# One branch around the overflow blocks, two norms from one pass of squares, and shifts on four buffers

## The reference, cut to what matters

```python
h = h + hier_moe(rms_norm(h, norm2_gain[l]), ...)      # end of the first block
x = rms_norm(h, final_gain)                            # EPS = 1e-6
# second block, for each of its two layers
shift, scale, gate = split(silu(c) @ w_mod + b_mod, 3)
hh = rms_norm_2(x, g, 1e-6) * (1.0 + scale) + shift
y = short_conv_mixer(hh, ...)        # layer 0: four projections, a 3-wide convolution, gates
y = dilated_mixer(hh, ...)           # layer 1
x = x + gate * y
```

## Time and profile before

| | us |
|---|---|
| median of 3 runs | 1616.34 (1616.0 to 1616.87) |
| the profiled execution's own time | 1616.23 |
| its span, first to last instruction | 1614.1 |
| PE busy in the span | 1447.2 (90%) |
| DVE busy | 705.7 (44%) |
| ACT busy | 488.8 (30%) |

### The profile page before, as it was taken

One profiled execution on the slowest core, in us unless ns is written; L12 is line 12 of the kernel. 1 busy time (PEld: TensorE's weight loads), 2 busy tenths in 40 slices (PEclk: granted clock), 3 DMA queues, 4 the chain that ended last, 5 costly groups with the idle time before them and its releaser, 6 DMA issues.

```text
span 1614.1 us, 18013 instructions
## 1 busy us (share of the span) xinstructions
PE 1447.2 (90%) x6858; PEld 1006.7 (62%) x6858; DVE 705.7 (44%) x1297; ACT 488.8 (30%) x723; POOL 38.6 (2%) x73
## 2 busy tenths in 40 slices
PE   6999997999898988898818999998999999999986
PEld 5786776444443433343216888776888888888765
DVE  4567737211011021010054756455256666666635
ACT  6462532110010100010043222324244445444532
POOL 2010000000000000000020110000000000000000
PEclk9999997999999999999959999998999999999988
DMA  8737335699999964999873553121212121121101
GB/s 355 310 131 263 139 119 209 276 426 426 427 426 427 427 268 163 391 423 429 351 296 131 196 208 131 65 80 53 105 53 105 53 85 73 52 105 52 53 1 65
DMA packets 36811, 336.88 MB, mean 209 GB/s; under 512 B 4560, under 2 KB 4688, under 8 KB 18384
## 3 DMA queue, kind: packets, MB, share of 16 engines
q1 hardware_dynamic: 29632, 304.69, 47.0%
q0 software_dynamic: 6624, 29.89, 5.2%
q10 hardware_dynamic: 432, 0.60, 0.1%
HBM read 312.62 MB, written 22.54 MB: 208 GB/s over the span
## 4 chain that ended last, share of the span: by engine, by line
PE 51%; DVE 2%; issue 2%; ACT 2%; DMA 2%; POOL 0%; DVEq 0%; SPq 0%; ACTq 0%; POOLq 0%
PE ps L290 50%; DMA spare<-in_wts_dram 1%; PE ps L718 1%; ACT ar L860 1%; DVE b_NL L1293 0%; PE ps L296 0%; DMA ar<-y_scratch,rt 0%; DVE ar L1285 0%; ACT b_NH L869 0%; DVE ar L1959 0%; DVE ar L1244 0%; DVE hres L1769 0%; DMA y_scratch<-gate 0%; POOL ar L2035 0%; ACT ar L1214 0%
## 5 line engine op out<-in xcount | busy, mean ns | idle before, releaser
L290 PE MATMUL ps<-ring,ar 128*64 128x512 f32 x800 | 244.3, 610 | 15.8 <-issue 10.7
L290 PE MATMUL ps<-ar 128*64 128x512 f32 (+5 forms) x798 | 231.4, 482 | 18.3 <-DVE ar L1589 6.8
L290 PE MATMUL ps<-b_NH,b_WH 128*128 128x512 f32 x704 | 185.6, 399 | 11.0 <-ACT b_NH L869 5.9
L290 PE MATMUL ps<-b_NH,b_WL 128*128 128x512 f32 x704 | 180.2, 391 | 0.0
L1226 DVE TENSOR_TENSOR b_WL<-ring,b_WH 128x1024 fp32r<-128x1024 f32 x112 | 136.6, 1220 | 94.5 <-ACT b_WH L812 94.5
L290 PE MATMUL ps<-b_NL,b_WH 128*128 128x512 f32 x704 | 174.4, 390 | 0.0
L812 ACT ACTIVATE b_WH<-ring 128x1024 fp32r<-128x1024 f32 x112 | 118.3, 1057 | 161.7 <-PE ps L290 159.9
L290 PEld LDWEIGHTS ps<-ar 128*64 128x64 f32 (+3 forms) x798 | 97.5, 163 | 100.5 <-issue 93.1
L290 PEld LDWEIGHTS ps<-b_NH,b_WH 128*128 128x128 f32 x704 | 129.7, 189 | 39.5 <-ACT b_NH L869 11.7
L290 PEld LDWEIGHTS ps<-ring,ar 128*64 128x64 f32 x800 | 77.8, 140 | 118.6 <-issue 117.0
L290 PEld LDWEIGHTS ps<-b_NH,b_WL 128*128 128x128 f32 x704 | 133.0, 189 | 27.9
(11 more groups left out here) (269 smaller groups left out, 1879.5 us busy)
## 6 DMA issues: line engine op xcount, KB each, us to landing
ring<-in_wts_dram SPq DMA_DIRECT2D x84, 2048.0 KB, 13.6
ar<-in_wts_dram SPq DMA_DIRECT2D x24, 2048.0 KB, 19.4
spare<-in_wts_dram SPq DMA_DIRECT2D x24, 2048.0 KB, 19.0
ring<-in_wmod_dram SPq DMA_DIRECT2D x24, 512.0 KB, 4.9
ar<-in_wmod_dram POOLq DMA_DIRECT2D x24, 512.0 KB, 4.1
y_scratch<-gate POOLq DMA_DIRECT2D x11, 1024.0 KB, 21.3
y_scratch<-gate SPq DMA_DIRECT2D x44, 128.0 KB, 15.7
y_scratch<-ar SPq DMA_DIRECT2D x24, 128.0 KB, 15.9
```

The costliest lines, as they stand in the source:

```text
L290: return pe.matmul(o, l, m, start=start, stop=stop, skip_group_check=True)
```

## The change

Four edits, and what they bring with them.

- **One branch.** On each engine the 12 `If(n_over > j)` go inside one `If(n_over > 0)`.
- **Both norms from one pass of squares.** ACT squares `hres` once for each p into `x0c`. DVE (`products`) multiplies these squares with the squared gain `fgsq` and sums, which gives the second mean without the first norm: 1/rs2 = sqrt(mean(h² g²) + EPS·mean(h²) + EPS²). ACT takes the root of that, DVE inverts it (`both`), and `x0c` is `hres` scaled by it (ACT for p = 0, 1, 2, DVE for p = 3). The final gain is folded into the scale columns (`C_FG`, `fgc`, once, where the columns are made). The first norm of `hres` itself, still wanted for the residual, is made later: four means and inverses ahead of the shift, and the four multiplications (`normed`) between the weight parts of the first panel of the convolution. The memsets of `TT` move behind them.
- **Shifts on four buffers.** `shifted(k)` waits for the low part of k - 4, and is issued two steps ahead. Both uses.
- **`fgr` earlier.** SP loads it behind the store of expert 28; ACT squares it into `fgsq`.

```diff
-            for j in range(NOV):
-                with pe.If(n_over > j):
...
+            with pe.If(n_over > 0):
+                for j in range(NOV):
+                    with pe.If(n_over > j):
+                        overflow(j)
...
             def turned_shift(ops, l, natural, tb, nb, tmps):
                 def shifted(k):
-                    o, src = tmps[k % 2], ps[:, k, :]
+                    o, src = tmps[k % 4], ps[:, k, :]
...
-                    if k >= 2:
-                        act.wait_ge(S["nl"], nb + k - 1)
+                    if k >= 4:
+                        act.wait_ge(S["nl"], nb + k - 3)
...
+                shifted(1)
                 for k in range(8):
-                    if k % 2 == 0:
-                        shifted(k + 1)
-                        act.wait_ge(S["ttd"], 4 * l + k // 2 + 1)
-                    else:
-                        act.wait_ge(S["tta"], 4 * l + k // 2 + 1)
-                    act.activation(ops[0][:, k, :], tmps[k % 2], ACT.Copy).then_inc(S["nh"], 1)
+                    if k % 2 == 1 and k < 7:
+                        shifted(k + 2)
+                    act.wait_ge(S[("ttd", "tta")[k % 2]], 4 * l + k // 2 + 1)
+                    act.activation(ops[0][:, k, :], tmps[k % 4], ACT.Copy).then_inc(S["nh"], 1)
...
+            act.wait_ge(S["fgain"], 16)
...
+            act.activation(fgsq, fgr, ACT.Square).then_inc(S["fgsq"], 1)
...
+            pk_squares(0)
+            pk_squares(1)
+            pk_root(0, rs2, 6)
+            pk_unit(0)
+            pk_squares(2)
+            pk_root(1, rs2, 6)
+            pk_unit(1)
+            pk_squares(3)
+            pk_root(2, rs2, 6)
+            pk_unit(2)
+            pk_root(3, rs2, 6)
+            for p in range(4):
+                pk_root(p, rs, 10)
...
+            def products(p):
+                dve.wait_ge(s_un[p], U_PK + 3)
+                dve.tensor_scalar(eps_s[:, p:p + 1], rs[:, p:p + 1], EPS / D, EPS * EPS, ALU.mult,
+                                  ALU.add).then_inc(s_un[p], 1)
+                dve.tensor_tensor_reduce(out=x0c[:, p, :], in0=x0c[:, p, :], in1=fgsq, scale=1.0, scalar=0.0,
+                                         op0=ALU.mult, op1=ALU.add, accum_out=rs2[:, p:p + 1]).then_inc(s_un[p], 1)
+                dve.wait_ge(s_un[p], U_PK + 5)
+                dve.scalar_tensor_tensor(out=rs2[:, p:p + 1], in0=rs2[:, p:p + 1], scalar=1.0 / D,
+                                         in1=eps_s[:, p:p + 1], op0=ALU.mult, op1=ALU.add).then_inc(s_un[p], 1)
+            def both(p):
+                dve.wait_ge(s_un[p], U_PK + 7)
+                dve.reciprocal(rs2[:, p:p + 1], rs2[:, p:p + 1]).then_inc(s_un[p], 1)
...
             pick(1, 1)
-            norm(0)
+            dve.wait_ge(S["fgsq"], 1)
+            products(0)
             pick(2, 0)
+            both(0)
             pick(2, 1)
-            norm(1)
+            products(1)
             pick(3, 0)
+            both(1)
             pick(3, 1)
+            products(2)
+            both(2)
+            products(3)
+            both(3)
+            dve.wait_ge(s_un[3], U_PK + 8)
+            dve.tensor_scalar(x0c[:, 3, :], hres[:, 3, :], rs2[:, 3:4], None, ALU.mult).then_inc(s_un[3], 1)
+            for p in range(4):
+                mean_square(p, rs, U_PK + 8)
+            for p in range(4):
+                inverse(p, rs, U_PK + 8)
...
+                        if q == 0 and c == 0:
+                            normed(j)
...
+                if n == NE - 4:
+                    sp.wait_ge(S["m_row"], NE // 4)
+                    sp.dma_start(fgr, row(R_FG, 1024)).then_inc(S["fgain"], 16)
```

More of the change, by code:

```diff
@@ L36 @@
 v_w0 v_w1
-cc tt0 xr cv y zc tm
+cc tt0 xr cv y zc tm fgsq fgc
 sw ra rb qk z vk scr att fl pt av
@@ L228, in program @@
         yg = [area(1024 * j, 1024) for j in range(8)]
-        fgr = area(8192, 1024)
+        fgr, fgsq = area(8192, 1024), area(9216, 1024)
+        eps_s = sm[:, 32:36]
         yTc = area(0, 8, 512)
@@ L641, in tensor_program, with overflow @@
             down_main(NE - 1)
[L642 to L659 removed]
+            def overflow(j):
+                if j == 0:
+                    pe.wait_ge(S["t_y"], NE)
+                pe.wait_ge(S["t_oh"], NE + j + 1)
+                pick_third(3).then_inc(S["t_gx"], 1)
+                pe.wait_ge(S["t_xg"], NE + j + 1)
+                turn_third(6).then_inc(S["t_tx"], 1)
+                pe.wait_ge(S["t_xt"], NE + j + 1)
+                pe.wait_ge(S["v_w0"], 32 * j + 16)
+                pe.wait_ge(S["v_w1"], 16 * j + 16)
+                up(xT3, 0, ov).then_inc(S["t_up"], 1)
+                pe.wait_ge(S["t_hh"], NE + j + 1)
+                turn_h(hh3, 6).then_inc(S["t_d1"], 1)
+                pe.wait_ge(S["t_ht"], NE + j + 1)
+                pe.wait_ge(S["v_w0"], 32 * j + 32)
+                down(hT3, 1, ov[0]).then_inc(S["t_d2"], 1)
+                pe.wait_ge(S["t_y"], NE + j + 1)
+            with pe.If(n_over > 0):
+                for j in range(NOV):
+                    with pe.If(n_over > j):
+                        overflow(j)
             pe.wait_ge(S["m_y"], NE)
             pe.wait_ge(S["t_y"], NE)
[L664 removed]
+            turn(x0c, U_PK + 9, banks_of(T_CV))
             for c in range(2):
@@ L1057, in scalar_program @@
             result(NE - 1)
-            for j in range(NOV):
-                with act.If(n_over > j):
-                    third_block(NE + j)
+            with act.If(n_over > 0):
+                for j in range(NOV):
+                    with act.If(n_over > j):
+                        third_block(NE + j)
             hi(P_C0, 0)
@@ L1749, in vector_program @@
                     weigh(g + 2)
-            for j in range(NOV):
-                with dve.If(n_over > j):
-                    third_block(NE + j, NE * CAP + CAP * (NE + j))
+            with dve.If(n_over > 0):
+                for j in range(NOV):
+                    with dve.If(n_over > j):
+                        third_block(NE + j, NE * CAP + CAP * (NE + j))
             dve.wait_ge(S["m_gx"], NE)
@@ L1770, in pick, with normed @@
                                          in1=hres[:, p, :], op0=ALU.mult, op1=ALU.add).then_inc(s_un[p], 1)
[L1772 to L1775, removed]
+            def products(p):
[10 more added lines that the diff above has]
+                dve.reciprocal(rs2[:, p:p + 1], rs2[:, p:p + 1]).then_inc(s_un[p], 1)
+            def normed(p):
+                dve.wait_ge(s_un[p], U_PK + 12)
                 dve.scalar_tensor_tensor(out=hres[:, p, :], in0=hres[:, p, :], scalar=rs[:, p:p + 1], in1=fgr,
@@ L2022, in gpsimd_program @@
             n_over, third = read_ctl(pool)
-            for j in range(NOV):
-                with pool.If(n_over > j):
-                    pool.wait_ge(S["ty"], 32 * (NE + j + 1))
+            with pool.If(n_over > 0):
+                for j in range(NOV):
+                    with pool.If(n_over > j):
+                        pool.wait_ge(S["ty"], 32 * (NE + j + 1))
             pool.wait_ge(S["ovx"], 1)
@@ new lines, in overflow, with expert @@
+            def overflow(j):
+                sp.wait_ge(S["ovx"], 1)
+                e0_ = sp.value_load(ctl[0:1, 1 + j:2 + j], min_val=P_MOE, max_val=P_MOE + 3 * NE - 3)
+                def expert(s, k):
+                    return sp.dma_start(ov[s], A["wts"][bass.ds(e0_ + k, 1), :, :].rearrange("o p c -> p (o c)"))
+                if j == 0:
+                    sp.wait_ge(S["m_d2"], NE)
+                    sp.wait_ge(S["t_d2"], NE)
+                else:
+                    sp.wait_ge(S["t_d2"], NE + j)
+                expert(0, 0).then_inc(S["v_w0"], 16)
+                expert(1, 1).then_inc(S["v_w1"], 16)
+                sp.wait_ge(S["t_up"], NE + j + 1)
+                expert(0, 2).then_inc(S["v_w0"], 16)
+                sp.wait_ge(S["t_y"], NE + j + 1)
+                store(2 * NE + j, ysb3, "ty")
+                sp.wait_ge(S["ty"], 32 * (NE + j + 1))
@@ L2130, in sync_program @@
+            with sp.If(n_over > 0):
+                for j in range(NOV):
+                    with sp.If(n_over > j):
+                        overflow(j)
             sp.wait_ge(S["m_d2"], NE)
             sp.wait_ge(S["m_y"], NE)
-            sp.wait_ge(S["m_hh"], NE)
             for j in range(3):
@@ L2135, in sync_program @@
             sp.wait_ge(S["ty"], 32 * NE)
-            sp.dma_start(fgr, row(R_FG, 1024)).then_inc(S["fgain"], 16)
             sp.wait_ge(s_yg[7], 16)
```

101 lines of the change are left out of this document (30 added, 71 removed).

## The result

| | before | after |
|---|---|---|
| median, us | 1616.61 of 4 (1616.0 to 1622.22) | 1596.97 of 4 (1591.69 to 1601.61) |
| ratio, 95% interval | | 0.9887 (0.9862 to 0.9913) |
| the profiled execution | 1616.23, span 1614.1 | 1591.69, span 1590.0 |

The changed kernel is 19.6 us faster by the medians and 24.1 by the two profiled spans.

What follows compares the result with a forecast made beforehand. PE was taken to be held by its overflow branches (35.5 us gap), closely by the norm chain, then the shift; 8.5 + 0.5 + 4.6 + 2.9 = 16.5 off 1616.23 gave 1599.7 us, range 1595.5 to 1604.5.

Steps and rivals of the forecast that it cites:

- The branch at nothing: PE's one remaining overflow branch, behind the experts: 0.22 to 5.77 us, some 20 us before the data, priced at nothing.
- (1): Rival: PE's far branch walks through all skipped pages at the same price as before: 1606.7 us; chance 6%.
- (2): Rival: PE's far branch walks through all skipped pages, each dearer than now: 1623 us; chance 3%.
- The norms: DVE's norm chain behind the gather: the last scaled unit of `x0c` ends at 838.7 us instead of 841.94.
- The feared surcharge for two different tensors: DVE's product with sum now reads two different tensors: 1.20 us from below, 1.28 from above.
- The 0.5 that the sum took for the gain's load: Loading `fgr` earlier spares the gather 1.2 us, of which 0.5 us counts as further gain in the chain.
- The turn: PE's transposes, 8 not 32 behind the last unit: first shift starts at 839.6 instead of 848.14, 8.5 us gained.
- The first shift: Four buffers, first shift to first tile: 17.5 us against 22.1, 4.6 gained, with 2.3 us for a 1.2 GHz stretch.
- The second shift: Four buffers in the second layer, shift to first tile: 18.1 us before, 2.9 us gained (2.0 to 3.9).
- `normed`, `fgr`, `fgc` at nothing: Moved work hidden behind weight parts, weight queue and experts, at no cost; `normed` without cover up to 5.1 us.
- (3): Rival: PE's clock stays at 1.2 GHz through both lead panels, DVE's hand-overs dear: 1604.5 to 1608 us; chance 8%.
- (4): Rival: the norm chain is not shortened, last unit at 841.94 as before: 1603 us; no chance given.

Runs made afterwards that it cites:

- the last experiment: The changed kernel run once more with no edit, on one chip with before: 1596.63 us of 4, ratio 0.987.
- the kernel whose clock was up: The changed kernel with the 12 separate overflow branches put back on PE alone: 1603.71 us, ratio 0.9932.

## Why the prediction was right

**The sum.** Predicted 1599.7 (1595.5 to 1604.5), measured 1596.97 and, once more, 1596.63. From the stages of the profiled pair the change is worth 16.17 + (18.07 - 15.37) = 18.9 us, against 16.5 predicted; the medians say 19.6 and 20.0. The other 5.2 us of the span's 24.1 are 1.75 in the last experts, 0.7 between first tile and second shift and 2.8 in the rest, all of which scatter by as much between kernels that don't differ there (for the rest see the last experiment). The forecast was 2.4 us short: 1.5 in the chain up to the shift and 1.1 in the first shift were taken too dear, 0.2 in the second too cheap.

**The branch at nothing: right.** It was put between 0.22 and 5.77 us, some 20 us ahead of the data. It takes 3.95 us and ends 19.9 us ahead. Rivals (1) and (2) stood on a walk through the skipped pages; with double the code it costs 4.06 us. The Trainium skill, "Runtime: NRT & Kernel Launch", section "Instruction fetch mechanics", has a taken branch fetch its target's page: the traces agree, one branch, one fetch, whatever lies between.

**The norms: right in kind, 1.9 us too dear.** From the end of the experts to the last scaling 838.7 - 808.07 = 30.6 us were predicted, and 28.73 measured. From the start of the fourth pick on, the chain was put at 838.7 - 823.97 = 14.73 and takes 13.78, the same in all nine kernels with the new norms. Nearly all of that difference is `products`: put at 1.63 for each group, the first group's runs from 822.46 to the next pick at 823.87 in the timeline, 1.41, because the small instructions overlap the product: 0.9 for four. The feared surcharge for two different tensors is nil, 1.22 us as in the earlier trace rows.

The other 1.0 us is the fourth pick itself, which starts 14.94 us behind the experts where the prediction kept the 15.90 of before. The 0.5 that the sum took for the gain's load would have to lie here, and no run shows it: the fourth pick starts 14.94 to 15.80 behind the experts in the eight executions with the early load and 15.69 in the one with new norms and the late load. That part of the gain may be luck of this execution.

**The turn: right.** The shift was expected 0.9 us behind the last scaling and came 0.85 behind it. With the chain this makes 10.5 us for 9.0 (8.5 and 0.5); in the second profiled execution of the changed kernel, 40.07 - 30.17 = 9.9.

**The first shift: right, 1.1 us too dear.** Predicted 17.5, with 15.2 if the clock were up and 2.3 for a stretch at 1.2 GHz; measured 16.40, and 15.04 in the kernel whose clock was up. The stretch was there, as expected, and costs 1.4 us here, not 2.3; over the eight kernels with one branch and four buffers the shift takes 16.06 to 17.19, 1.0 to 2.2 above the 15.04.

**The second shift: right.** 15.2 predicted, 15.37 measured; 14.1 to 15.4 over all kernels with four buffers, close to the bounds of the prediction (14.2 to 16.1). The clock goes with it: the granted clock stays at 1.2 GHz until 5.5 to 6.3 us behind the start of the shift in the three kernels with 15.0 to 15.4, and until 1.2 to 2.1 us behind it in the six with 14.1.

**`normed`, `fgr`, `fgc` at nothing: right.** In after's waits of PE from 740 to 900 us none is for low parts of weights (`b_WL`), nor is one from 852 to 1080, which takes in the second panel. Without that cover the four multiplications cost 4.6 us at the shift, where the prediction had said up to 5.1.

**Rivals (3) and (4).** The clock at 1.2 GHz through both lead panels did not come: it was low for 3.4 us in the first one, and in the second stretch, of 15.3 us, its mean was 0.80. That the chain would not shorten fell too: the last scaling comes 28.7 us behind the experts, before the change 841.94 - 808.07 = 33.9 us.

## What to carry to other kernels

Look at what comes next before you price a wait: the gap of 35.5 us was worth 5.6 alone, because the norm chain ended only 1.6 us ahead of it, and only all three edits together gave 16 us. Where PE skips a row of blocks, one condition around all of them cost one fetch of some 4 us here, over 12 blocks or 24. When executions of one kernel scatter by more than an edit is worth, compare the length of the edited stage between two fixed instructions in each trace, and undo one part at a time to see whether the parts add up. Cut the stage where its scatter ends: from the fourth pick on, the norm chain repeated to 0.02 us, while the medians of 4 executions could not tell 5 us in the stage.

## What the runs showed of the hardware that was not expected

With the additional transposes PE's clock was up and fell again in the gap ahead of the lead panel: in the kernel with 48 of them PE was busy 2.18 of 5.0 us at a granted clock of 1.00, stood still for 2.38 us up to 843.35, and the 7 us from 843 on, with PE busy 6.39, ran at 0.51. Keeping PE busy ahead of such a gap bought nothing here: the transposes ran at 2.4 GHz (eight in 1.09 us), but the low stretch in the lead panel grew from 3.4 to 7 us, and there a matmul takes 0.63 us instead of 0.39.
